# Experts of a hybrid decoder: empty slots left out of gather and store, results put at the place of their pair

## The chip, the cores and the metric

One core of a Trainium2 chip runs the whole program. The metric is the device time of one execution in microseconds, the median of the runs shown. TensorE (PE), VectorE (DVE), ScalarE (ACT), GpSimd (POOL) and SyncE (SP) run their own instruction streams and meet at semaphores. SP and ACT issue DMAs through hardware queues, POOL through the software queue; all of them are moved by the core's 16 DMA engines.

## The reference, cut to what matters

Two layers work on a residual stream of 1024 tokens by 1024 numbers, all float32. Each layer is a mixer (latent attention and a gated delta rule in layer 0, retention in layer 1), a residual norm, and a mixture of 32 experts with another residual norm. The change concerns the experts only:

```python
def routed_experts(xt, expert_id, weights, w_gate, w_up, w_down):   # xt (1024, 1024), 2 experts a token
    ...
    counts = jnp.zeros((N_EXPERTS,), jnp.int32).at[flat_e].add(1)
    padded = (counts + MOE_BLOCK - 1) // MOE_BLOCK * MOE_BLOCK         # MOE_BLOCK = 128
    start = jnp.cumsum(counts) - counts
    pstart = jnp.cumsum(padded) - padded
    slot = pstart[e_sorted] + (jnp.arange(n, dtype=jnp.int32) - start[e_sorted])
    ...
    xb = xt[slot_tok].reshape(n_blocks, MOE_BLOCK, D)

    def expert_block(args):
        xs, e = args
        hid = jax.nn.silu(xs @ w_gate[e]) * (xs @ w_up[e])             # 1024 -> 512
        return hid @ w_down[e]                                         # 512 -> 1024

    yb = lax.map(expert_block, (xb, block_expert)).reshape(n_slots, D)
    contrib = yb[slot] * w_sorted[:, None].astype(yb.dtype)
    return jax.ops.segment_sum(contrib, tok_sorted, num_segments=T)
```

So 2048 pairs of token and expert are computed, each weighted and added to its token.

## The kernel before, in words

`build` runs the stages one after the other; each is a block of its own that ends with a barrier of all engines. `moe` (line 2598 on) runs four of them for each layer, tagged f0 and f1: `modulate`, `route`, `experts`, `combine`.

`route` (line 2001) computes the logits, picks the two experts of each token and gives each pair a slot. Slots come in blocks of 128; block e belongs to expert e, and blocks 32 to 47 are spare for experts with more than 128 pairs. The slots of a block are filled from its first one. Then 16 pairs of one-hot tiles A and B, each with a matmul into pk (line 2075), put token + 1 at the place of its slot: pk has the slot within the block on its partition and the block on its column; an empty slot holds 0. From it DVE makes `full` (does the block hold more than 64 rows, line 2193), and `token` (line 2194 on), where an empty slot asks for token 0. `route`'s SP loads the first experts' weights beside that.

`experts` (line 2239) walks over the blocks in groups of four (QUAD), as many as `used` says. For a block v:

- SP loads gate and up weights (`load_gu`, lines 2224 and 2225, 2 MB each) into one of four buffers, then the down weights of block v - 3 (`load_d`, line 2229, two times 1 MB) into one of two buffers.
- POOL (`gather`, lines 2323 and 2326) copies the column of tokens and issues an indirect DMA that fetches 128 rows of x, 4 KB each, into one of two buffers, once the transposes of block v - 2 are through.
- PE runs gates(v), hid_turn(v - 1), turn(v + 1), downs(v - 1), in this order. turn transposes the gathered rows, gates multiplies by gate and up, hid_turn transposes the hidden rows, downs multiplies by the down weights. gates and downs work on two halves s of 64 rows; the second is left out where `full` is 0. Within a half, the two column halves of the result lie on partitions 0 to 63 and 64 to 127.
- ACT and DVE apply the modulation (lines 2441 and 2488), the Silu, the product, and copy the down projection into y (128 x 2 x 512; ACT line 2457 for s = 0, DVE line 2509 for s = 1). So y[64 c + t, s, :] is columns 512 c on of the row 64 s + t.
- ACT waits for both copies and stores y with two DMAs of 256 KB (line 2461) at the block's place in y_dram (`expert_rows`).

`combine` (line 2533) reads, for each tile of 128 tokens, the two rows of each token from y_dram with indirect DMAs from POOL (line 2555, four tiles of buffers), multiplies them on PE by diagonal weights (line 2579), and ends with the residual norm: DVE lines 1598 to 1624, ACT, and on POOL the bias (line 1643). POOL asks for tile t + 4 ahead of its own work on tile t. SP loads x and stores the result (`traffic`, in order: x of tile t, then the store of tile t - 3 once its bias is added).

`attention` (line 788), in layer 0, also stores zeros over the 16 spare blocks of y_dram (lines 826 and 831), so that they can be read.

## Time and profile before

| | us |
|---|---|
| median of the runs | 3794.65 |
| lowest and highest of 3 runs | 3790.22 and 3802.92 |
| the profiled execution | 3790.52 |
| its span, first to last instruction | 3788.7 |
| experts of layer 0, first to last PE instruction, about | 1201 to 1798 |
| experts of layer 1, the same | 3109 to 3698 |
| PE busy over the span | 3229.5 (85%) |

How the rows are read. In a row of the slices, each digit is the busy share of a slice of 94.7 us in tenths. A row of the groups has line, engine, operation, output<-inputs, size, count, then busy us, mean ns of one, idle time of the engine before them and who ended it. A row of busy times by stretch has the stretch, its length, then busy us and count of PE, PE's weight loads, DVE, ACT and POOL, the granted clock as a share of full speed, the DMA engines' mean busy share and GB/s. A row of the timeline has start, length, engine, line, what was done, count, and in brackets the idle time before it and who ended that. A row of the DMA issues has the issuing queue, the count, KB each and the median us from issue to landing. A matmul of float32 appears as two records.

### The profile page before, as it was taken

Reading aid. Unit: us, or ns where it says so; the run is one execution under the profiler, and the core shown is the slowest. Engines: PE = TensorE matmul, PEld = TensorE weight load, DVE = VectorE, ACT = ScalarE, POOL = GpSimd, SP = SyncE. Lnnn points to the kernel's source line nnn. Section 1 sums busy time; section 2 is a strip of 40 time slices with the busy share of each in tenths; the row PEclk is TensorE's granted clock in tenths of the full one; section 3 lists DMA queues with packets and bytes.
Section 4 is the critical chain, followed back from the end, with each engine's and each line's share of the span. In section 5 each row is a group of like instructions: output and inputs, shape, how many; then the busy total and the mean of one; then the engine's idle time right before and its main releaser. Section 6 shows DMA issues by size and latency. Waiting matters only on the chain. (4 is left out here: it accounts for less than half of the span.)

```text
span 3788.7 us, 44646 instructions
## 1 busy us (share of the span) xinstructions
PE 3229.5 (85%) x15035; PEld 1782.1 (47%) x15036; DVE 1274.6 (34%) x3073; ACT 908.2 (24%) x1749; POOL 503.7 (13%) x866
## 2 busy tenths in 40 slices
PE   7978889677865999999479899999989759988884
PEld 5656654367434434333146565655644343433331
DVE  4665554354243112221623232232311241121226
ACT  1022224123120111111135354453410011111111
POOL 0000010166010000000301111111100100000003
PEclk9879999778885999999689999999989859999997
DMA  7722001122235999996530202010030157899985
GB/s 283 270 87 84 0 23 34 49 65 47 89 104 230 388 367 411 425 426 236 214 111 1 67 0 67 0 45 22 0 122 34 60 230 300 329 427 424 426 358 200
DMA packets 195570, 668.26 MB, mean 176 GB/s; under 512 B 46863, under 2 KB 97770, under 8 KB 162414
## 3 DMA queue, kind: packets, MB, share of 16 engines
q1 hardware_dynamic: 162574, 579.56, 39.5%
q0 software_dynamic: 14144, 51.39, 3.5%
q10 hardware_dynamic: 18720, 35.66, 2.5%
q8 instruction: 70, 1.15, 0.1%
q14 instruction: 62, 0.51, 0.0%
HBM read 605.17 MB, written 61.37 MB: 176 GB/s over the span
## 5 line engine op out<-in xcount | busy, mean ns | idle before, releaser
L1805 PE MATMUL ret_pqkv<-ret_w,hT_mix 128*128 128x512 f32 x1024 | 457.6, 600 | 20.0 <-DMA ret_w<-in_ret_w_in_dram 20.0
L2354 PE MATMUL f0e_pgu<-f0w_gu,f0e_xT 128*64 128x512 f32 x1568 | 344.8, 596 | 7.0 <-issue 3.2
L1678 PE MATMUL mo_py<-mo_w,mixT 128*128 128x512 f32 x768 | 333.4, 597 | 4.8 <-DMA mo_w<-in_ret_w_out_dram 2.5
L1805 PEld LDWEIGHTS ret_pqkv<-ret_w,hT_mix 128*128 128x128 f32 x1024 | 192.6, 193 | 240.1 <-issue 239.9
L2354 PE MATMUL f1e_pgu<-f1w_gu,f1e_xT 128*64 128x512 f32 x1344 | 296.0, 595 | 7.4 <-issue 3.6
L1678 PEld LDWEIGHTS mo_py<-mo_w,mixT 128*128 128x128 f32 x768 | 147.0, 192 | 192.6 <-issue 184.8
L1813 PE MATMUL ret_pgate<-ret_w,hT_mix 128*128 128x256 f32 x1024 | 231.6, 379 | 0.0
L2354 PEld LDWEIGHTS f0e_pgu<-f0w_gu,f0e_xT 128*64 128x64 f32 x1568 | 125.4, 138 | 220.9 <-issue 220.8
L2373 PE MATMUL f1e_pd<-f1w_d,f1e_hidT 128*64 128x512 f32 x672 | 173.1, 668 | 52.6 <-DMA f1w_d<-in_moe_w_down_dram 51.3
L1813 PEld LDWEIGHTS ret_pgate<-ret_w,hT_mix 128*128 128x128 f32 x1024 | 189.9, 190 | 25.0 <-issue 1.9
L2354 PEld LDWEIGHTS f1e_pgu<-f1w_gu,f1e_xT 128*64 128x64 f32 x1344 | 104.2, 138 | 194.1 <-issue 194.0
L2373 PE MATMUL f0e_pd<-f0w_d,f0e_hidT 128*64 128x512 f32 x784 | 176.9, 600 | 7.4 <-DMA f0w_d<-in_moe_w_down_dram 5.5
L434 PE MATMUL gc_pq<-hT_mix,gc_w 128*128 128x512 f32 x384 | 168.3, 597 | 10.1 <-DMA gc_w<-in_hy_w_in_dram 10.1
L1960 DVE TENSOR_TENSOR ret_state<-ret_state,ret_pout 128x256 f32<-128x256 f32 x56 | 23.5, 421 | 406.2 <-PE ret_pout L1837 406.2
L2502 DVE COPY f0e_hidT<-f0e_ph 128x512 f32<-128x512 f32 x32 | 22.1, 691 | 363.7 <-PE f0e_ph L2366 363.3
L2502 DVE COPY f1e_hidT<-f1e_ph 128x512 f32<-128x512 f32 x32 | 22.1, 691 | 359.0 <-PE f1e_ph L2366 359.0
L1790 POOL TENSOR_TENSOR ret_z<-ret_z,ret_head_gain 128x256 f32<-128x256 f32 x64 | 46.5, 726 | 700.5 <-DVE ret_z L1971 700.5
L2373 PEld LDWEIGHTS f1e_pd<-f1w_d,f1e_hidT 128*64 128x64 f32 x672 | 53.0, 153 | 149.4 <-issue 93.5
L434 PEld LDWEIGHTS gc_pq<-hT_mix,gc_w 128*128 128x128 f32 x384 | 73.4, 192 | 102.3 <-issue 91.9
L1879 ACT COPY ret_v<-ret_pqkv 128x256 f32<-128x256 f32 x64 | 23.8, 372 | 389.1 <-PE ret_pqkv L1805 389.1
L1598 DVE TENSOR_TENSOR mo_z<-mo_py,mo_gate_b 128x1024 f32<-128x1024 f32 x16 | 19.6, 1225 | 272.0 <-PE mo_py L1678 272.0
L2373 PEld LDWEIGHTS f0e_pd<-f0w_d,f0e_hidT 128*64 128x64 f32 x784 | 58.3, 138 | 102.7 <-issue 94.2
(547 smaller groups left out, 4705.4 us busy)
## 6 DMA issues: line engine op xcount, KB each, us to landing
f0w_gu<-in_moe_w_gate_dram SPq DMA_DIRECT2D x32, 2048.0 KB, 11.3
f0w_gu<-in_moe_w_up_dram SPq DMA_DIRECT2D x32, 2048.0 KB, 16.8
f0w_d<-in_moe_w_down_dram SPq DMA_DIRECT2D x64, 1024.0 KB, 15.8
f1w_gu<-in_moe_w_gate_dram SPq DMA_DIRECT2D x32, 2048.0 KB, 25.5
f1w_gu<-in_moe_w_up_dram SPq DMA_DIRECT2D x32, 2048.0 KB, 30.5
f1w_d<-in_moe_w_down_dram SPq DMA_DIRECT2D x64, 1024.0 KB, 24.9
mixT<-in_ada_w_dram SPq DMA_DIRECT2D x80, 512.0 KB, 5.6
expert_rows<-f0e_y ACTq DMA_DIRECT2D x64, 256.0 KB, 10.4
```

The costliest lines, as they stand in the source:

```text
L434: mm = pe.matmul(pq[u][:, half * 512:(half + 1) * 512], w[u][:, kk, :], g.hT[:, kk, half * 512:(half + 1) * 512], start=(kk == 0), stop=(k ...
L1598: dve.tensor_tensor(z[:, :], y, self.gate_b[:, :], ALU.mult).then_inc(S["zmul"], 1)
L1678: mm = pe.matmul(py[t % 3][:, half * 512:(half + 1) * 512], mixT[:, kk, t * P:(t + 1) * P], ws[:, kk, half * 512:(half + 1) * 512], start= ...
L1790: pool.tensor_tensor(zb, zb, head_gain[u][:, :], ALU.mult).then_inc(S["gained"], 1)
L1805: mm = pe.matmul(p_qkv[s % 2][:, :], g.hT[:, kk, t * P:(t + 1) * P], w[u][:, kk, 0:512], start=(kk == 0), stop=(kk == KD - 1))
L1813: mm = pe.matmul(p_gate[s % 2][:, 0:RDV], g.hT[:, kk, t * P:(t + 1) * P], w[u][:, kk, 512:W], start=(kk == 0), stop=(kk == KD - 1))
L1879: act.copy(v[b][:, :], p_qkv[s % 2][:, QK:512])
L1960: ch.mark(dve.tensor_tensor(st[:, :], state[(s - 1) % 2][:, :], p_out[:, RDV:2 * RDV], ALU.add))
L2354: mm = pe.matmul(pgu[s][half * HALF:(half + 1) * HALF, :], xT[u % 2][:, kk, s * HALF:(s + 1) * HALF], ew.gu[u][:, :, kk, half * FH:(half + ...
L2373: mm = pe.matmul(pd[s][half * HALF:(half + 1) * HALF, :], hidT[:, s, k % 2, k // 2, :], ew.d[u % 2][:, k, half * DH:(half + 1) * DH], star ...
L2502: dve.tensor_copy(hidT[:, :, :, :, :].rearrange("p s j h t -> p (s j h t)"), ph[:, :])\
```

## The change

`route` numbers the second pair of a token T higher than the first, so that a slot knows its pair (token, or 1024 + token) and not only its token; an empty slot gets an index out of bounds. The tokens for the gather are made from that. PE turns the pairs with four small matmuls, so that each partition of y finds the row and the column half that it belongs to (`dest`, twice the pair plus the half). In `experts`, the gather skips indices out of bounds; the two buffers are set to 0 once ahead of the loop. ACT's two stores go. POOL instead issues, after the gather for block v, two indirect stores for block v - 4, one for each s, with rows of 512 numbers; they too skip indices out of bounds. y_dram has 2048 rows, one for each pair. In `combine` the indirect gathers are plain loads from SP, issued ahead of x of the same tile. The zeros in `attention` go, with their memset.

```diff
@@ attention
-            sp.wait_ge(blanked, 1)
-            for i in spare:
-                sp.dma_start(g.y_dram[i * P:(i + 1) * P, :], blank[:, :]).then_inc(cleared, 16)
-            sp.wait_ge(cleared, 16 * len(spare))
...
-            pool.memset(blank[:, :], 0.0).then_inc(blanked, 1)
@@ route, tensor
+            pe.wait_ge(S["paired"], 1)
+            for s_ in range(2):
+                for c in range(2):
+                    mm = pe.matmul(pl[c * 64:c * 64 + 64, s_ * NBLK:(s_ + 1) * NBLK], g.ident[:, s_ * 64:s_ * 64 + 64],
+                                   pairf[:, :], start=True, stop=True, skip_group_check=True)
+            mm.then_inc(S["dealt"], 1)
@@ route, vector
-            ch.do(dve.tensor_copy(tok[:, :], tok_i[:, :]))
+            ch.do(dve.tensor_copy(tok[:, 0, :], tok_i[:, :]))
+            ts(tok[:, 1, :], tok[:, 0, :], float(T), None, ALU.add)
+            ts(low_half[:, :], tok[:, 0, 0:1], P // 2 + 0.5, None, ALU.is_gt)
...
             ts(r.full[:, :], pk[64:65, 0:NBLK], 0.5, None, ALU.is_gt)
-            ch.do(dve.memset(tokf[:, :], 0.0))
-            ts(tokf[:, 0:NBLK], pk[:, 0:NBLK], -1.0, 0.0, ALU.add, ALU.max)
+            ts(pairf[:, :], pk[:, 0:NBLK], 0.5, float(4 * PAIRS), ALU.is_lt, ALU.mult)
+            dve.scalar_tensor_tensor(out=pairf[:, :], in0=pk[:, 0:NBLK], scalar=-1.0, in1=pairf[:, :],
+                                     op0=ALU.add, op1=ALU.add).then_inc(S["paired"], 1)
+            dve.wait_ge(S["paired"], 1)
+            ch.do(dve.memset(tokf[:, :], float(4 * PAIRS)))
+            ts(tokf[:, 0:NBLK], pairf[:, :], T - 0.5, float(-T), ALU.is_gt, ALU.mult)
+            tt(tokf[:, 0:NBLK], tokf[:, 0:NBLK], pairf[:, :], ALU.add)
             ch.do(dve.tensor_copy(r.token[:, :], tokf[:, :]))
+            dve.wait_ge(S["dealt"], 1)
+            ts(r.dest[:, :, :].rearrange("p s n -> p (s n)"), pl[:, 0:2 * NBLK], 2.0, low_half[:, 0:1], ALU.mult, ALU.add)
@@ experts, gpsimd
                 pool.indirect_dma_start(out=xg[b][:, :], out_offset=None, in_=x_dram,
-                                        in_offset=bass.IndirectOffsetOnAxis(ap=idx[b][:, :], axis=0))\
+                                        in_offset=bass.IndirectOffsetOnAxis(ap=idx[b][:, :], axis=0),
+                                        bounds_check=T - 1, oob_is_err=False)\
                     .then_inc(pairs["x_in"][b], 16)
+            def scatter(m, u, dst):
+
+                k, b = turns(m, u, 0)
+                pool.wait_ge(S["ya"], m * QUAD + (u + 1))
+                pool.wait_ge(S["yb"], m * QUAD + (u + 1))
+                reach(pool, pairs["stored"][b], k * 32)
+                pool.tensor_copy(didx[b][:, :], dst).then_inc(pairs["didxd"][b], 1)
+                pool.wait_ge(pairs["didxd"][b], k + 1)
+                pool.sem_inc(S["asked"], 1)
+                for s in range(2):
+                    pool.indirect_dma_start(out=yd, out_offset=bass.IndirectOffsetOnAxis(ap=didx[b][:, s:s + 1], axis=0),
+                                            in_=y[b][:, s, :], in_offset=None, bounds_check=2 * PAIRS - 1, oob_is_err=False)\
+                        .then_inc(pairs["stored"][b], 16)
+
+            for b in range(2):
+                pool.memset(xg[b][:, :], 0.0).then_inc(S["blanked"], 1)
+            pool.wait_ge(S["blanked"], 2)
             for u in range(QUAD):
                 gather(0, u, tk[:, 0:1, u])
             with pool.Fori(1, quads_used(pool)) as m:
                 for u in range(QUAD):
                     gather(m, u, tk[:, bass.ds(m, 1), u])
+                    scatter(m - 1, u, dest[:, bass.ds(m - 1, 1), u, :].rearrange("p a s -> p (a s)"))
             end = quad_last(pool)
             gather(end + 1, 0, tk[:, bass.ds(end + 1, 1), 0])
+            for u in range(QUAD):
+                scatter(end, u, dest[:, bass.ds(end, 1), u, :].rearrange("p a s -> p (a s)"))
@@ experts, scalar
-                act.wait_ge(S["ya"], m * QUAD + (u + 1))
-                act.wait_ge(S["yb"], m * QUAD + (u + 1))
-                for c in range(2):
-                    act.dma_start(yd[bass.ds(k, 1), b, c].rearrange("a t s n -> (a t) s n"),
-                                  y[b][c * HALF:(c + 1) * HALF, :, :]).then_inc(pairs["stored"][b], 16)
@@ combine
-            rn.traffic(sp)
+            def load_rows(t):
+                if t >= NR:
+                    sp.wait_ge(summed, t - NR + 1)
+                for k in range(2):
+                    sp.dma_start(rows[k][t % NR][:, :], y_dram[k * T + t * P:k * T + (t + 1) * P, :])\
+                        .then_inc(r_in[t % NR], 16)
+
+            for t in range(NT + 3):
+                if t < NT:
+                    load_rows(t)
+                    rn.load_x(sp, t)
+                if t == 1:
+                    rn.load_rows(sp)
+                if t >= 3:
+                    rn.store(sp, t - 3)
+            sp.wait_ge(rn.S["stored"], 16 * NT)
...
-                    pool.indirect_dma_start(out=rows[k][t % NR][:, :], out_offset=None, in_=y_dram,
-                                            in_offset=bass.IndirectOffsetOnAxis(ap=r.slot[:, t, k:k + 1], axis=0))\
-                        .then_inc(r_in[t % NR], 16)
@@ build
-    g.y_dram = nc.dram_tensor("expert_rows", [NBLK * P, D], F32).ap()
+    g.y_dram = nc.dram_tensor("expert_rows", [PAIRS, D], F32).ap()
```

## Rows read from the trace of the kernel before

**Rows 1.** The slices of the page: the DMA engines.

```profile
DMA  7722001122235999996530202010030157899985
```

**Rows 2.** The groups of instructions: the down projections of layer 0 and layer 1.

```profile
L2373 PE MATMUL f0e_pd<-f0w_d,f0e_hidT 128*64 128x512 f32 x784 | 176.9, 600 | 7.4 <-DMA f0w_d<-in_moe_w_down_dram 5.5 <-DVE f0e_hidT L2502 1.3
...
L2373 PE MATMUL f1e_pd<-f1w_d,f1e_hidT 128*64 128x512 f32 x672 | 173.1, 668 | 52.6 <-DMA f1w_d<-in_moe_w_down_dram 51.3 <-DVE f1e_hidT L2502 1.0
```

**Rows 3.** Busy times by stretch, one in layer 0 and two in layer 1.

```profile
1600.00:1700.00 100.00, 99.66 (x490) 40.17 (x488) 20.17 (x48) 16.45 (x41) 6.90 (x12) 1.00 1.01 425
3210.00:3310.00 100.00, 98.93 (x478) 39.46 (x475) 14.32 (x33) 11.83 (x30) 4.61 (x8) 1.00 0.84 333
3310.00:3670.00 360.00, 305.84 (x1405) 120.00 (x1405) 74.49 (x176) 60.42 (x154) 25.29 (x44) 0.93 1.00 422
```

**Rows 4.** The timeline of PE in layer 1: two down projections that follow one another.

```profile
3576.11 5.35 PE L2373 MATMUL f1e_pd<-f1w_d,f1e_hidT 128*64 128x512 f32 x16 [3.62 <-DMA f1w_d<-in_moe_w_down_dram]
...
3593.36 5.32 PE L2373 MATMUL f1e_pd<-f1w_d,f1e_hidT 128*64 128x512 f32 x16 [3.45 <-DMA f1w_d<-in_moe_w_down_dram]
```

**Rows 5.** The DMA issues: weights and stores of layer 1's experts, x of its combination.

```profile
f1w_gu<-in_moe_w_gate_dram SPq DMA_DIRECT2D x32, 2048.0 KB, 25.5
...
f1w_d<-in_moe_w_down_dram SPq DMA_DIRECT2D x64, 1024.0 KB, 24.9
...
expert_rows<-f1e_y ACTq DMA_DIRECT2D x64, 256.0 KB, 9.1
...
f1c_x<-x SPq DMA_DIRECT2D x8, 512.0 KB, 4.5
```

**Rows 6.** The timeline at the end of layer 1's route.

```profile
3103.30 1.09 PE L2075 MATMUL f1r_pk<-f1r_B,f1r_A 128*128 128x48 f32 x4 [0.17 <-DVE f1r_B L2178]
...
3107.41 0.20 DVE L2090 TENSOR_SCALAR f_full<-f1r_pk 1x48 int32<-1x48 f32 x1
...
3108.07 0.19 DVE L2196 CAST f_token<-f1r_tokf 128x52 int32<-128x52 f32 x1
```

**Rows 7.** The timeline: the memset in attention, and the first gather of layer 1's experts.

```profile
280.37 0.95 POOL L831 MEMSET at_blank<- 128x1024 f32 x1 [273.52 <-POOLq L94]
...
3110.29 1.02 POOL L2326 DMA_INDIRECT f1e_xg<-x,f1e_idx  x1 [0.84 <-POOL f1e_idx L2323]
...
3122.10 1.97 PE L2348 MATMUL f1e_px<-ident,f1e_xg 128*128 128x128 f32 x8 [9.06 <-DMA f1e_xg<-x,f1e_idx]
```

**Rows 8.** The tiles f1e_y (stores), then f1e_xg (gathers): time from issue to landing.

```profile
DMA to landing us min/median/max: 3.1/9.1/14.0
...
DMA to landing us min/median/max: 4.2/11.1/12.3
```

**Rows 9.** The timeline at the end of layer 1's experts and the start of the combination.

```profile
3699.27 1.42 ACTq L2461 DMA_DIRECT2D expert_rows<-f1e_y  x2
...
3706.49 0.81 SPq L1545 DMA_DIRECT2D f1c_x<-x  x2
```

**Rows 10.** The timeline of layer 1's combination: PE, DVE's first step of tiles, SP.

```profile
3708.33 3.78 PE L1572 MATMUL f1c_py<-f1c_diag,ones 128*128 128x512 f32 x4 [9.95 <-DVE f1c_diag L1565]
3718.73 19.55 PE L2579 MATMUL f1c_py<-f1c_r,f1c_weights 128*128 128x512 f32 x40 [6.62 <-DMA f1c_r<-expert_rows,f_slot]
...
3724.58 1.23 DVE L1598 TENSOR_TENSOR f1c_z<-f1c_py,f1c_gate_b 128x1024 f32<-128x1024 f32 x1 [13.17 <-PE f1c_py L2579]
...
3733.14 1.22 DVE L1598 TENSOR_TENSOR f1c_z<-f1c_py,f1c_gate_b 128x1024 f32<-128x1024 f32 x1
...
3741.31 0.34 SPq L1550 DMA_DIRECT2D out_dram<-f1c_z  x1
...
3745.43 1.22 DVE L1598 TENSOR_TENSOR f1c_z<-f1c_py,f1c_gate_b 128x1024 f32<-128x1024 f32 x1
...
3755.23 1.22 DVE L1598 TENSOR_TENSOR f1c_z<-f1c_py,f1c_gate_b 128x1024 f32<-128x1024 f32 x1 [3.06 <-PE f1c_py L2579]
...
3768.78 1.22 DVE L1598 TENSOR_TENSOR f1c_z<-f1c_py,f1c_gate_b 128x1024 f32<-128x1024 f32 x1 [1.26 <-PE f1c_py L2579]
```

More of the change, by code:

```diff
@@ L804, in attention @@
         otok = g.sb(ctx, "at_o", [P, NT, 2 * VD])
-        blank = g.sb(ctx, "at_blank", [P, D])
-        blanked, cleared = g.sems(ctx, "at", "blanked", "cleared")
-        spare = range(NE, NBLK)
         nmax = g.sb(ctx, "at_nmax", [P, NI])
@@ L1989, in __init__ @@
         self.weight = g.sb(ctx, f"{tag}_weight", [P, NT, 2])
-        self.slot = g.sb(ctx, f"{tag}_slot", [P, NT, 2], I32)
+        self.dest = g.sb(ctx, f"{tag}_dest", [P, 2, NBLK], I32)
         self.token = g.sb(ctx, f"{tag}_token", [P, NBLK + QUAD], I32)
@@ L2012, in route @@
         iota = sb("iota", [P, P])
-        tok = sb("tok", [P, NT])
+        tok = sb("tok", [P, 2, NT])
+        low_half = sb("low_half", [P, 1])
+        slot = sb("slot", [P, NT, 2], I32)
+        pairf = sb("pairf", [P, NBLK])
         gm, gs, gi, m1, m2, i1, i2, ex, tw = (sb(n, [P, NT]) for n in "gm gs gi m1 m2 i1 i2 ex tw".split())
@@ L2037, in route @@
         pk = g.ps(ctx, f"{tag}_pk", [P, 512])
-        names = "w_in b_in iotas logits steps grp gexp diff dexp onehot ranked hit placed".split()
+        names = "w_in b_in iotas logits steps grp gexp diff dexp onehot ranked hit placed paired dealt".split()
         S = dict(zip(names, g.sems(ctx, tag, *names)))
@@ L2249, in experts @@
         idx = [sb(f"idx{u}", [P, 1], I32) for u in range(2)]
+        didx = [sb(f"didx{u}", [P, 2], I32) for u in range(2)]
         xg = [sb(f"xg{u}", [P, D]) for u in range(2)]
@@ L2259, in experts @@
         pd = [g.ps(ctx, f"{tag}_pd{s}", [P, 512]) for s in range(2)]
-        names = "xt_a xt_b xa xd gu_a gu_b silu_a silu_b hid_a hid_b ht hTd down_a down_b ya yb asked left".split()
+        names = "xt_a xt_b xa xd gu_a gu_b silu_a silu_b hid_a hid_b ht hTd down_a down_b ya yb asked left blanked".split()
         S = dict(zip(names, g.sems(ctx, tag, *names)))
-        pairs = {n: g.sems(ctx, tag, n + "0", n + "1") for n in "idxd x_in stored".split()}
+        pairs = {n: g.sems(ctx, tag, n + "0", n + "1") for n in "idxd didxd x_in stored".split()}
         block = ctx.enter_context(nc.Block())
@@ L2546, in _ @@
         def _(sp):
-            rn.traffic(sp)
+            def load_rows(t):
[13 more added lines that the diff above has]
+            sp.wait_ge(rn.S["stored"], 16 * NT)
         @block.gpsimd
         def _(pool):
-            def gather(t):
-                if t >= NR:
-                    pool.wait_ge(summed, t - NR + 1)
-                for k in range(2):
-                    pool.indirect_dma_start(out=rows[k][t % NR][:, :], out_offset=None, in_=y_dram,
-                                            in_offset=bass.IndirectOffsetOnAxis(ap=r.slot[:, t, k:k + 1], axis=0))\
-                        .then_inc(r_in[t % NR], 16)
-            for t in range(NR):
-                gather(t)
             for t in range(NT):
-                if t + NR < NT:
-                    gather(t + NR)
                 rn.pool(pool, t)
```

11 lines of the change are left out of this document (6 added, 5 removed).

## The prediction, made before the change was run

> **What bounds the kernel now.** I began with the slices of the page: the DMA engines are full in two stretches, late in each layer's experts [rows 1]. The groups of instructions come next. In layer 0 the down projection's matmuls (line 2373) waited 5.5 us for their weights, in layer 1 51.3 us; everything else that the experts' matmuls wait for is a few us [rows 2]. A half of a block is 16 of these matmul records, so 784 are 49 halves and 672 are 42: 32 blocks in each layer, of which 17 and 10 hold more than 64 rows. The busy times by stretch say where the two engines trade places [rows 3]. Between 1600 and 1700 the DMA moves 425 GB/s at a share of 1.01 and PE is busy 99.66 us of 100: both are full. From 3210 to 3310 PE is full and the DMA is not. From 3310 to 3670 the DMA is full (422 GB/s) and PE is idle for 54 us of 360. There the start of a block's down projection follows the one before by 17.25 us, with 3.5 us of it a wait for weights [rows 4]. A block's transfers explain this period: gate and up 2 x 2048 KB, down 2 x 1024 KB, stores 2 x 256 KB [rows 5], and the gather of 128 rows of 4 KB, 512 KB. That is 7168 KB = 7.34 MB, and 7.34 MB / 426 GB/s = 17.2 us. So bytes taken away are worth time in that stretch of layer 1; in layer 0 they are worth at most the 5.5 us.
>
> **How much traffic goes.** 2048 pairs lie in 32 x 128 = 4096 slots, so half of the gathered and of the stored rows are dropped: on average 256 KB + 256 KB of a block's 7168 KB, 7.1%. What that is worth depends on how it falls on the 16 DMA engines. The full slots are always the first of a block, so the dropped rows are the high partitions. If the kept rows spread evenly, the stretch shrinks by 7.1% of 360 us = 25.7 us. If each engine serves fixed partitions, the engines with the low partitions keep their whole gather (no block's first rows are empty), and the weights are complete only when the last engine has its share. The scatter is different: a row of 1024 numbers lies as two halves of 512 on partitions t and 64 + t, and the two column tiles s hold the tokens below and above 64. So its kept rows lie in both halves of the partitions, and an engine drops at least most of s = 1: the store falls by about half on every engine. Then 256 of 7168 KB go, 3.6%, 12.9 us. Below these lies a third bound, nothing, if a dropped row costs an engine what a kept one does. No row shows an indirect transfer with dropped rows. I take the middle, 12.9 us: a wait for a whole tile ends with its last engine, and [rows 3] has all engines full before, so the fullest sets the pace afterwards. For layer 0 I take 5 of the 5.5 us.
>
> The Trainium skill, "DMA: Bandwidth & Descriptors", section "The descriptor swizzle", says that a transfer to 128 partitions puts partitions 0 to 63 on engines 0 to 7 and the rest on 8 to 15, four neighbouring partitions to an engine. By it the gather's saving is all on engines that nobody waits for, and the sum is the one I forecast; without it, it would be some 13 us less. No row before the change shows single engines.
>
> **What is added ahead of the experts.** At the end of route DVE has one instruction more before the pairs are known (two for pairf, where one made tokf), and then PE turns pairf with 4 matmuls, 8 records, while DVE makes the tokens (memset, two more steps, cast). Four records of 48 columns took 1.09 us and DVE's small steps come every 0.24 us [rows 6]. So PE starts three steps (0.75 us) after the first of these, the one for the full flags, needs 2 x 1.09 us, and one more DVE step (dest) follows: with 0.1 us of hand-over some 3.3 us. Before, DVE's last step ended 0.85 us after the flags' began. That is +2.4 us in each layer, 4.8 in all, and nothing covers it, because the stage's barrier waits for DVE. The two early steps on tok and low_half lie under the wait for the logits: nothing.
>
> Then two memsets of 128x1024 stand ahead of the first gather on POOL. One such memset took 0.95 us [rows 7], so the gather is issued 1.9 us later. But the gather took 11.8 us to its first use, beside 4 MB of weights issued with it (9.8 us at 426 GB/s), where 4.2 us is its shortest landing [rows 8]. It shares the engines with weights that run out first, so between 0 and 1.9 us appear. I take 1 us a layer, 2 in all.
>
> **Inside the loop.** POOL gets a second wait, for the y of the block four before, behind which the next gather is queued. That y is copied just after the transposes that release the gather ahead of it, and the next gather waits for transposes a block later, so it is not held up. POOL's work per block grows from 0.97 us plus a copy to three indirect DMAs and two copies, with the pauses ahead of them about 5.3 of 17 us, covered. The y buffers are needed again two blocks (34 us) after the scatter is asked for; the longest landing of a store was 14.0 us [rows 8]. Nothing on both. ACT loses 1.42 us of issuing per block and never was late: nothing.
>
> **The end of the experts.** ACT issues its last stores at 3699.27, the next stage's first instruction comes at 3706.49 [rows 9]. Now POOL copies the indices (0.19), pauses 0.84 as it did ahead of a gather [rows 7], and issues two indirect DMAs of 0.97 with 0.3 between: the second starts 2.1 us after where ACT's first did, that is 1.4 after ACT's second. The shortest landing of a store from ACT was 3.1 us, of an indirect gather 4.2 us [rows 8]: +1.1. Sum 2.5 us a layer, bounds 1 and 8 (a landing like the gather's median of 11.1); I take 2.5 since nothing else moves then. 5 in all.
>
> **The combination.** Before, PE was through with the gate rows at 3712.1 and waited until 3718.73 for rows that POOL had asked for [rows 10]. Direct loads on SP take 0.43 us to issue and 4.5 us to land, as x does [rows 5], so both rows of tile 0 are there at about 3712 and PE begins 6.5 us earlier. Against that stands SP's order. Tile t + 4 used to be asked for by POOL ahead of its own work on tile t; now it stands on SP behind the store of tile t, which waits for that work. DVE begins tile 2 at 3733.14, and the store of tile 0 goes out at 3741.31, 8.2 us later [rows 10]. The store and the two loads are 1.5 MB, some 5.3 us to the last landing (4.5 us for 0.5 MB, and about 1 MB more, less overlap), and PE took 5.85 us for a tile from cold (3718.73 to 3724.58). So DVE has tile 4 19.4 us after it began tile 2, where its own work for two tiles takes 12.3 us (3733.14 to 3745.43): 7.1 us late, once for tiles 4 and 5 and once for 6 and 7. Before, DVE went from tile 0 to tile 7 in 44.2 us, with waits of 3.06 and 1.26 us. Without them 39.9, and with two of 7.1 it is 54.1: 9.9 us lost against 6.5 won, about +3 a layer, 6 in all. The bounds of one layer are -3 (loads land in 3.6 us less each) and +6.
>
> **The attention.** The zeros for the spare blocks go: 16 stores and one memset of 0.95 us that ends before the weights it could delay have landed. The store stream lies beside PE-bound work: nothing, at most 0.5 us gained.
>
> **The sum.** Added: 4.8 + 2 + 5 + 6 = 17.8 us. Saved: 12.9 + 5 = 17.9 us. The profiled execution took 3790.52 us (its span 3788.7), so the same execution would take 3790.4. It was the lower end of the runs, 4.1 us under their median of 3794.65; the after kernel's runs should scatter alike, and halfway between the two bases is 3792.5.
>
> **The rivals.** (a) The dropped rows spread evenly: layer 1 saves 25.7 instead of 12.9, so 3792.5 - 12.8 = 3779.7. For it speaks that the indices are read one by one when the transfer is made, so that what is left could be dealt out. Against it, that both the indices and the tile lie by partition, and that a fixed split by partition is the simplest one that gives the full, even share of [rows 3] for full tiles. The rows can't decide; I give the fixed split the larger part. (b) Slower: a dropped row stays as an entry that an engine must work through at the price of a kept one, in the gather and in the scatter. Then the stretch from 3310 does not shrink, none of the 17.9 us comes, and the 17.8 us of added steps stand: 3810.4. It decides as soon as less than some 6 us are saved in all, for then the sum is above +0.3%. For it speaks only that the transfers' number of instructions and their completion count stay; against it, that the bounds check exists to leave rows out. That the change doesn't do what it says is this case. (c) The mechanism of the forecast, but the combination's reload is quicker and starts cleaner: 6 less, 3786; or the stores' tail longer: 5 more. These lie in the forecast's own range, 3783 to 3803.
>
> **How the numbers follow.** Forecast (middle case) 0.5, (a) 0.3, (b) 0.2. A measurement of this kernel can tell about 0.3%, 11.4 us, from no change: the lines are at 3783.3 and 3806.0. The forecast's case lies within them at 0.40, below at 0.05, above at 0.05. Case (a) sits 3.6 us beyond the lower line, so 0.19 of its 0.3 are faster and 0.11 the same. Case (b) is 0.16 slower and 0.04 the same. Together 0.24, 0.55, 0.21. The range reaches to both rivals: from 3775, a little under (a), since the combination's bound could add, to 3811, just above (b).
>
> **What would show it.** In layer 1, the period of the down projections between 3310 and 3670: 16.6 us in the forecast, 16.0 by (a), 17.2 by (b). The DMA share there: under 1.00 while PE still waits for f1w_d means uneven engines (about 0.96); 1.00 with a shorter stretch means (a); 1.00 and the same length (b). The packets of the software queue: about half of the gathers' 4 KB rows, none of the combination's, and the kept 2 KB halves. PE's wait for f0w_d should be near 0. Route should end 2.4 us later, the combination's first matmul of rows should come some 6 us sooner after the stage's start, with two waits of about 7 us for rows in each combination instead of the smaller ones. The prediction is wrong if the indirect stores hold POOL so long that gathers come late (PE would wait for f1e_xg inside the loop), or if their landings delay the copies of y.

## The result, and the profile after

The changed kernel takes 3819.52 us (median of 7 runs, 3808.09 to 3821.09), the kernel before beside it 3798.05 us (7 runs, 3790.22 to 3802.92). The ratio is 1.005, 95% interval 1.0038 to 1.0062: slower by 0.5%, some 19 us. The prediction, 3792.5 us with a range of 3775 to 3811, was wrong. Scaled to the median from which it was made, the ratio gives 3813.6, also above the range. The profiled execution took 3821.04 us, its span is 3819.3.

The page of the kernel after: the slices of the DMA engines, their packets, and the software queue (packets, MB, share).

```profile
DMA  7720001221235989993530202010030157799954
...
DMA packets 185075, 625.33 MB, mean 164 GB/s; under 512 B 55021, under 2 KB 105928, under 8 KB 151918
...
q0 software_dynamic: 19776, 33.62, 2.4%
```

Before, the packets had 668.26 MB, so 42.9 MB are gone. Two runs below put half of them back one by one: 17.8 MB are gathered rows (fullgather, 51.43 MB in this queue) and 16.8 MB stored rows (fullstore, 50.37 MB); the rest is the 8.4 MB of zeros for the spare blocks. So the rows were left out, and rival (b) can be asked directly: over the whole trace a packet of 4 bytes in this queue took 9 ns, one of 4096 bytes 162 ns in the mean. The groups of the down projections answer to [rows 2]; PE waits less for down weights in both layers, 1.7 us where it was 5.5 and 41.7 where it was 51.3:

```profile
L2409 PE MATMUL f1e_pd<-f1w_d,f1e_hidT 128*64 128x512 f32 x672 | 167.7, 650 | 45.4 <-DMA f1w_d<-in_moe_w_down_dram 41.7
...
L2409 PE MATMUL f0e_pd<-f0w_d,f0e_hidT 128*64 128x512 f32 x784 | 175.3, 596 | 3.6 <-DMA f0w_d<-in_moe_w_down_dram 1.7
```

PE's timeline in the stretch that the DMA bounds, two down projections that follow one another, as in [rows 4]:

```profile
3594.49 5.00 PE L2409 MATMUL f1e_pd<-f1w_d,f1e_hidT 128*64 128x512 f32 x16 [3.11 <-DMA f1w_d<-in_moe_w_down_dram]
3611.19 5.18 PE L2409 MATMUL f1e_pd<-f1w_d,f1e_hidT 128*64 128x512 f32 x16 [3.26 <-DMA f1w_d<-in_moe_w_down_dram]
```

The period is 16.70 us where it was 17.25; the forecast was 16.6. So the gain came. The loss is at the seams. Here is the timeline of the end of layer 1's experts and the start of its combination (GpSimd, SP, PE, VectorE's first step of tiles 0, 2, 4, 6 and 7), beside [rows 9] and [rows 10]:

```profile
3713.92 0.19 POOL L2352 COPY f1e_didx<-f_dest 128x2 int32 x1 [1.93 <-ACT f1e_y L2491]
3714.96 0.98 POOL L2356 DMA_INDIRECT expert_rows<-f1e_y,f1e_didx  x1 [0.86 <-POOL f1e_didx L2352]
3716.24 0.97 POOL L2356 DMA_INDIRECT expert_rows<-f1e_y,f1e_didx  x1 [0.30 <-issue]
3728.37 0.81 SPq L2580 DMA_DIRECT2D f1c_r<-expert_rows  x2
...
3730.14 3.78 PE L1564 MATMUL f1c_py<-f1c_diag,ones 128*128 128x512 f32 x4 [17.09 <-DVE f1c_diag L1557]
...
3733.07 1.17 SPq L2580 DMA_DIRECT2D f1c_r<-expert_rows  x2
3733.71 3.64 PE L2611 MATMUL f1c_py<-f1c_r,f1c_weights 128*128 128x512 f32 x8
...
3737.39 1.22 DVE L1590 TENSOR_TENSOR f1c_z<-f1c_py,f1c_gate_b 128x1024 f32<-128x1024 f32 x1 [4.17 <-PE f1c_py L2611]
...
3751.52 1.23 DVE L1590 TENSOR_TENSOR f1c_z<-f1c_py,f1c_gate_b 128x1024 f32<-128x1024 f32 x1 [5.34 <-PE f1c_py L2611]
...
3759.70 0.34 SPq L1542 DMA_DIRECT2D out_dram<-f1c_z  x1
3760.08 1.25 SPq L2580 DMA_DIRECT2D f1c_r<-expert_rows  x2
...
3765.62 6.51 PE L2611 MATMUL f1c_py<-f1c_r,f1c_weights 128*128 128x512 f32 x8 [10.71 <-DMA f1c_r<-expert_rows]
...
3772.18 1.22 DVE L1590 TENSOR_TENSOR f1c_z<-f1c_py,f1c_gate_b 128x1024 f32<-128x1024 f32 x1 [8.28 <-PE f1c_py L2611]
...
3792.77 1.23 DVE L1590 TENSOR_TENSOR f1c_z<-f1c_py,f1c_gate_b 128x1024 f32<-128x1024 f32 x1 [8.29 <-PE f1c_py L2611]
...
3798.33 1.22 DVE L1590 TENSOR_TENSOR f1c_z<-f1c_py,f1c_gate_b 128x1024 f32<-128x1024 f32 x1
```

Two things are to be seen. The second store of the last block is asked for at 3716.24 and the next stage starts 12.1 us later. And inside the combination VectorE waits three times for rows: 5.34, 8.28 and 8.29 us.

I cut both traces at the same instructions and took the difference after minus before, in us, layer 0 and layer 1:

| from ... to | layer 0 | layer 1 | both | forecast |
|---|---|---|---|---|
| first matmul of route to first transpose of gathered rows | +2.7 | +2.2 | +4.9 | +6.8 |
| from there to the last matmul of the down projections | -3.8 | -11.5 | -15.3 | -17.9 |
| from there to the first instruction of the combination | +7.9 | +7.2 | +15.1 | +5 |
| from there to VectorE's first step of tile 7 | +6.7 | +7.6 | +14.3 | +6 |
| sum | | | +19.0 | -0.1 |

The span grew by 30.6 us. Of the other 11.6 about 5 lie between the last matmul of layer 0's combination and the first of layer 1's route (1180.7 us before, 1185.8 after) and 4.5 ahead of the first route. The changed kernel's variants below have 1180.2 to 1183.5 us for the first of these. For the second, the trace of probe, which runs the kernel before's code up to there, has 1145.0 us where the kernel before has 1136.3. So I take both for scatter of one execution; the sum of the table agrees with the 19 us of the ratio.

The third row has a cause that the profile's views don't show, since they leave out what isn't work. The records as the profiler took them do (start in us, duration in ns). After, at the end of layer 1's experts:

```
  3713.27   5064 Scalar  EVENT_SEMAPHORE   (waits for the landing of the last stores)
  3714.96    977 GpSimd  DMA_INDIRECT
  3715.25   9965 GpSimd  DRAIN
  3716.24    973 GpSimd  DMA_INDIRECT
  3718.40      8 Scalar  DRAIN
```

Before:

```
  3659.50  10062 GpSimd  DRAIN
  3659.72    968 GpSimd  DMA_INDIRECT      (the last gather)
  3700.81   2427 Scalar  EVENT_SEMAPHORE   (waits for the landing of the last stores)
  3703.32      8 Scalar  DRAIN
```

In these records GpSimd's instruction stream ends a block of code with a drain. After, ScalarE has seen all stores landed at 3718.33, 2.1 us after the last was asked for, but GpSimd's drain ends at 3725.22, 9.0 us after, and the next stage's first instruction comes 3.2 us behind it (3728.37). Before, it came 3.3 us behind ScalarE's wait (3703.24, 3706.49): a drain of 10 us began behind the last gather and was over at 3669.56, under 28 us of TensorE work. The stores moved the last software DMA to the end of the stage, and with it the drain.

### The profile page after: what moved, and what is told of

Same layout as the page of the kernel before. It is cut to its first block and busy times, and to the rows that moved or that the text cites. A ratio compares the mean times of both kernels' runs of the same rounds, so it can differ in the third digit from the quotient of the medians.

```text
span 3819.3 us, 44971 instructions
## 1 busy us (share of the span) xinstructions
PE 3236.5 (85%) x15051; PEld 1790.7 (47%) x15052; DVE 1274.7 (33%) x3085; ACT 907.6 (24%) x1749; POOL 614.4 (16%) x1029
## 3 DMA queue, kind: packets, MB, share of 16 engines
q0 software_dynamic: 19776, 33.62, 2.4%
HBM read 605.17 MB, written 52.99 MB: 172 GB/s over the span
## 5 line engine op out<-in xcount | busy, mean ns | idle before, releaser
L1797 PE MATMUL ret_pqkv<-ret_w,hT_mix 128*128 128x512 f32 x1024 | 458.9, 602 | 20.3 <-DMA ret_w<-in_ret_w_in_dram 20.3
L2409 PE MATMUL f1e_pd<-f1w_d,f1e_hidT 128*64 128x512 f32 x672 | 167.7, 650 | 45.4 <-DMA f1w_d<-in_moe_w_down_dram 41.7
```

The source lines that it names most:

```text
L1797: mm = pe.matmul(p_qkv[s % 2][:, :], g.hT[:, kk, t * P:(t + 1) * P], w[u][:, kk, 0:512], start=(kk == 0), stop=(kk == KD - 1))
L2409: mm = pe.matmul(pd[s][half * HALF:(half + 1) * HALF, :], hidT[:, s, k % 2, k // 2, :], ew.d[u % 2][:, k, half * DH:(half + 1) * DH], star ...
```

## The experiments

Three theories. **1**: the end of the experts is late by GpSimd's drain, not by the landing of its stores. **2**: the combination is late because on SP the loads of rows stand behind stores that wait for GpSimd. **3**: the gather's missing rows save nothing, since they all lie on the same high partitions; the whole gain is the halved stores. The rival of the third is that missing rows help wherever they lie.

**tail**: the changed kernel, whose experts' stage ends without the drain; GpSimd's stores are still waited for by their semaphores.

```diff
-        block = ctx.enter_context(nc.Block())
+        block = ctx.enter_context(nc.Block(no_gpsimd_drain=True))
```

> The changed kernel, with one edit: the block of the experts ends without GpSimd's drain of its software DMAs. Theory 1: after the last indirect store POOL's drain holds the barrier, in the changed kernel from 3715.25 to 3725.22 us, although ACT saw the store landed at 3718.34. Then the next stage starts about 7 us sooner after the last down projection, in both layers: some 14 us less than the changed kernel, the time near 3805, ratio to the kernel before about 1.002. Rival: the barrier waits for the stores' landing or for clearing of semaphores; then nothing changes (3819, ratio 1.005).

Measured: 3801.45 us (10 runs), ratio to the kernel before 1.0007 (0.9993 to 1.0022), that is 18 us less than the changed kernel. The timeline of its end of layer 1's experts:

```profile
3705.22 0.97 POOL L2356 DMA_INDIRECT expert_rows<-f1e_y,f1e_didx  x1 [0.86 <-POOL f1e_didx L2352]
3706.49 0.97 POOL L2356 DMA_INDIRECT expert_rows<-f1e_y,f1e_didx  x1 [0.30 <-issue]
3711.84 0.81 SPq L2580 DMA_DIRECT2D f1c_r<-expert_rows  x2
```

From the last issue to the next stage 5.35 us instead of 12.13: 6.8 us in this layer; in layer 0 the time from the experts' last matmul to the combination's first fell from 17.6 to 11.6. Together 13 us of the 15.1; from the last matmul to the combination's first instruction 1.9 and 0.4 us remain over the kernel before. The other 5 of the 18 us lie within the two intervals, some 5 us each. Theory 1 holds: without the drain the next stage again begins 3.3 us after ScalarE has seen the landing (3708.58, 3711.84).

**probe**: the same cause put into the kernel before. Behind the last down projection GpSimd gathers one block that nobody uses, and waits for it.

```diff
             gather(end + 1, 0, tk[:, bass.ds(end + 1, 1), 0])
+            pool.wait_ge(S["ya"], end * QUAD + QUAD)
+            pool.wait_ge(S["yb"], end * QUAD + QUAD)
+            ...
+            pool.indirect_dma_start(out=xg[1][:, :], out_offset=None, in_=x_dram, ...)
+            pool.wait_ge(pairs["x_in"][1], end * 32 + 48)
```

> The kernel before with one thing added: behind the last down projection of each layer GpSimd gathers one more block of 128 rows by an indirect transfer and waits for its landing; nothing uses it. Theory 1 (the end of a block of code waits for GpSimd's drain, which takes about 10 us from the last indirect transfer on): the stage's end moves 7 us back in each layer, as in the changed kernel, median about 3811 (3806 to 3815), ratio 1.0025 to 1.0045, and GpSimd's drain record ends about 10 us after that gather. Rival (only the landing itself counts, about 4 us of which the ordinary stores' landings already cover 2 to 3): 1 to 2 us per layer, median 3800 to 3802.

Measured: 3806.32 us (10 runs), ratio 1.0024 (1.0012 to 1.0036), which is 9.3 us, less than the 14 of theory 1 and more than the rival's 4. In its trace the time from the experts' last matmul to the combination's first of rows went from 20.0 to 25.9 us in layer 0 and from 20.3 to 25.5 in layer 1. The records:

```
  3715.38    943 GpSimd  DMA_INDIRECT      (the added gather)
  3716.28   5281 Scalar  EVENT_SEMAPHORE   (waits for the landing of the last stores)
  3721.40     42 GpSimd  COMPARE_BRANCH    (the added gather has landed)
  3721.55   2840 GpSimd  DRAIN
```

The drain ends at 3724.39, again 9.0 us after the issue of the last indirect DMA. I had priced it by the changed kernel, where that DMA is asked for 3.8 us after the start of the last matmul; here it is 2.1 us. So the end by the drain is 11.1 us after the matmul, where before the stores' landing was seen 5.4 us after it (3697.8 to 3703.24): 5.7 us were to be expected, 5.2 and 5.9 came. Half of it the rival would claim: the ordinary stores landed 2.8 us later beside the added gather, at 3721.56, and the drain ended 2.8 us after that. So probe alone does not part the two causes; tail does. In the changed kernel, where the landing takes 2.1 us, the drain decides.

**rows**: the changed kernel; in the combination SP asks for the rows of tile t + 1 ahead of the store of tile t - 3.

```diff
+            load_rows(0)
             for t in range(NT + 3):
+                if t < NT - 1:
+                    load_rows(t + 1)
                 if t < NT:
-                    load_rows(t)
                     rn.load_x(sp, t)
```

> The changed kernel, with one edit: in the combination SP asks for the rows of tile t + 1 ahead of the store of tile t - 3, not behind it. Theory 2: the reload behind the store is what makes DVE wait 8.3 us twice in each combination (tiles 4 and 6). Then both waits fall to 0 to 3 us, each combination is 10 to 15 us shorter (from its start to DVE's tile 7: 69.9 us in the changed kernel, 62.3 before), and the time is near 3795, ratio 0.998 to 1.000. Rival: the loads themselves are slow (11.1 us from issue to landing for tile 2), because rows, x, gain and bias share one queue; then DVE's waits stay about as long and less than 5 us are won in all.

Measured: 3790.23 us (10 runs), ratio 0.9982 (0.9969 to 0.9995), 29 us less than the changed kernel. The timeline of its combination in layer 1:

```profile
3713.14 1.76 SPq L2580 DMA_DIRECT2D f1c_r<-expert_rows  x4
...
3715.77 0.95 SPq L2580 DMA_DIRECT2D f1c_r<-expert_rows  x2
...
3722.11 1.22 DVE L1590 TENSOR_TENSOR f1c_z<-f1c_py,f1c_gate_b 128x1024 f32<-128x1024 f32 x1 [4.12 <-PE f1c_py L2613]
...
3730.67 1.22 DVE L1590 TENSOR_TENSOR f1c_z<-f1c_py,f1c_gate_b 128x1024 f32<-128x1024 f32 x1
...
3753.37 1.23 DVE L1590 TENSOR_TENSOR f1c_z<-f1c_py,f1c_gate_b 128x1024 f32<-128x1024 f32 x1 [0.95 <-PE f1c_py L2613]
...
3767.81 1.22 DVE L1590 TENSOR_TENSOR f1c_z<-f1c_py,f1c_gate_b 128x1024 f32<-128x1024 f32 x1 [0.17 <-PE f1c_py L2613]
```

Shown are VectorE's first steps of tiles 0, 2, 5 and 7. The waits of 5.34, 8.28 and 8.29 us at tiles 2, 4 and 6 are gone; what is left is 0.95 at tile 5 and 0.17 at tile 7. Tile 7 comes 54.7 us after the stage's start, where it was 70.0 in the changed kernel and 62.3 before. The combination's matmuls of rows take 49.0 and 49.3 us where the changed kernel's take 62.7 and 63.7. Tile 2, too, is cured: its rows are now asked for at 3715.77, 2.6 us after the stage's start, ahead of tile 1's x, gain and bias, and not 4.7 us after it behind them. Theory 2 holds, and with it the other half of that edit: the direct loads let VectorE begin its first tile 9.0 us after the stage's start, where it was 18.1 [rows 9, 10].

**fullgather**: the changed kernel, but an empty slot fetches row 1023 of x. The stores still leave their rows out.

```diff
+            ts(tokf[:, :], tokf[:, :], float(T - 1), None, ALU.min)
```

> The changed kernel, but the empty slots fetch row 1023 instead of being skipped, so that every gather moves 128 rows of 4 KB. Theory 3 (fixed partitions): the engines with the low partitions had a full gather anyway, so the experts of layer 1 take the same time as in the changed kernel, 0 to 3 us more, with the DMA share back at 1.00. Rival, kept rows spread evenly: 3.6% of 360 us, about 13 us more in layer 1.

Measured: 3816.45 us (6 runs), ratio 1.0057 (1.0036 to 1.0078), no different from the changed kernel. Its period, from PE's timeline, is again 16.7 us:

```profile
3594.49 5.20 PE L2410 MATMUL f1e_pd<-f1w_d,f1e_hidT 128*64 128x512 f32 x16 [3.05 <-DMA f1w_d<-in_moe_w_down_dram]
3611.20 5.35 PE L2410 MATMUL f1e_pd<-f1w_d,f1e_hidT 128*64 128x512 f32 x16 [3.08 <-DMA f1w_d<-in_moe_w_down_dram]
```

The experts of layer 1 take 576.8 us (578.7 in the changed kernel). Half of every gather, left out or not, makes no difference where it lies now. (That all fill rows are the same row did not make them cheap: between 3400 and 3650 this queue's packets of 4096 bytes took 160 ns in the mean in both kernels.)

**fullstore**: the other half alone. The gather leaves rows out, but each empty slot's row is stored, to a spare row of its own that nothing reads.

```diff
-            ts(pairf[:, :], pk[:, 0:NBLK], 0.5, float(4 * PAIRS), ALU.is_lt, ALU.mult)
+            ts(pairf[:, :], pk[:, 0:NBLK], 0.5, None, ALU.is_lt)
+            tt(pairf[:, :], pairf[:, :], spare[:, :], ALU.mult)
...
```

> The changed kernel, but the rows of empty slots are stored after all, each to a spare row of its own behind those of the pairs (nothing reads them); the gather still leaves its empty rows out. Theory (all that the experts gained, 11.5 us in layer 1 and 3.8 us in layer 0 up to the last down projection, comes from the halved stores): layer 1's experts go from 578.7 to about 589 us (4.3 MB more at 422 GB/s are 10 us), layer 0's by 3, the median to about 3832 (3827 to 3838). Rival (the gain came from elsewhere, as from the stores leaving ScalarE's queue): experts within 3 us of 578.7, median 3818 to 3823.

Measured: 3831.83 us (4 runs), ratio 1.0089 (1.0073 to 1.0106).

```profile
3587.36 3.65 PE L2413 MATMUL f1e_pd<-f1w_d,f1e_hidT 128*64 128x512 f32 x16 [1.59 <-DMA f1w_d<-in_moe_w_down_dram]
3604.70 3.65 PE L2413 MATMUL f1e_pd<-f1w_d,f1e_hidT 128*64 128x512 f32 x16 [3.71 <-DMA f1w_d<-in_moe_w_down_dram]
```

The period is 17.3 us, what it was before the change, and the experts take 590.3 us in layer 1 (589.1 before the change) and 597.6 in layer 0 (595.3). From the first transpose of gathered rows to the last down projection, the second row of the table, it is 575.8 and 583.4 us, and 575.7 and 582.2 before. The whole gain was in the stores.

**spread**: the changed kernel with its gathered rows dealt over other partitions, so that the empty slots' rows are missing everywhere alike. The transposition was done as a product with a permutation matrix.

```diff
-                        mm = pe.transpose(px[half][:, j * P:(j + 1) * P], xg[b][:, kk:D:KD], g.ident[:, :])
+                        mm = pe.matmul(px[half][:, j * P:(j + 1) * P], xg[b][:, kk:D:KD], g.perm[:, :],
+                                       start=True, stop=True)
...
```

> The changed kernel, with the gathered rows dealt to other partitions: slot 16 a + e goes to partition 64 (e >> 3) + 32 (a >> 2) + 4 (e & 7) + (a & 3), and PE multiplies by the permutation where it multiplied by the identity, so that the result is the same. Theory 3, an engine serves fixed partitions in groups of four, as the page says: then the kept rows now fall evenly on the 16 engines, the fullest engine drops about half of its gather, and layer 1's experts get shorter by another 3.6% of 360 us, 10 to 13 us; the DMA share in the stretch where PE waits rises from 0.95 to 1.00. Rival: the gather was spread evenly already, or nothing was uneven: 0, or 0.5 us more for the added step in route.

Measured: 3955.03 us (5 runs), ratio 1.041 (1.0385 to 1.0435): this run can't decide its question. The groups of instructions, of this kernel and then of the changed one:

```profile
L2392 PE MATMUL f1e_px<-perm,f1e_xg 128*128 128x128 f32 x528 | 130.9, 402 | 10.0 <-DMA f1e_xg<-x,f1e_idx 10.0
L2392 PEld LDWEIGHTS f1e_px<-perm,f1e_xg 128*128 128x128 f32 x528 | 128.2, 334 | 12.4 <-DMA f1e_xg<-x,f1e_idx 11.6 <-issue 0.8
```

```profile
L2384 PE MATMUL f1e_px<-ident,f1e_xg 128*128 128x128 f32 x264 | 36.0, 280 | 10.2 <-DMA f1e_xg<-x,f1e_idx 10.2
L2384 PEld LDWEIGHTS f1e_px<-ident,f1e_xg 128*128 128x128 f32 x264 | 33.1, 195 | 12.6 <-DMA f1e_xg<-x,f1e_idx 11.8 <-issue 0.8
```

A float32 product with a permutation matrix takes two records where a float32 transpose takes one, and each is 1.4 times as long: 95 us more of PE busy time in each layer, which hides what the deal may bring.

**spread2**: the same idea without a load on PE. Slot 32 a + q is gathered to partition 4 q + a, the transpose stays, and the copies that follow it put the columns back in order.

```diff
-                    ins = act.activation(xT[u % 2][:, j, :], px[0][:, j * P:(j + 1) * P], ACT.Identity,
+                    ins = act.activation(dealt(xT[u % 2], j), there(px[0], j), ACT.Identity,
...
+        def dealt(tile, j):
+            return tile[:, j, :].rearrange("p (a q) -> p a q", a=4)
+        def there(bank, j):
+            return bank[:, j * P:(j + 1) * P].rearrange("p (q a) -> p a q", a=4)
...
```

> Again a deal of the gathered rows over other partitions, this time at no cost for TensorE: the slot numbered 32 a + q of a block (a from 0 to 3, q from 0 to 31) is gathered to partition 4 q + a, the transposition stays as it is, and ScalarE's and VectorE's copies of its result put the columns back in the order of the slots. The column of tokens is moved to the same partitions by one small matmul in the route. So the empty slots' rows are missing on all parts of the partitions alike. Theory 3 (gathered rows saved nothing because the missing ones all lay on the same partitions, whose DMA engines idle while the fullest still carry all their rows): layer 1's experts, now 578.7 us, end about 9 us sooner (4.4 MB fewer at 422 GB/s are 10 us), layer 0's 1 to 3 us sooner, route 0.5 us later per layer: median about 3809 (3804 to 3813), ratio to the kernel before 1.002 to 1.004. Rival (bytes of the gather are hidden anyway, or a missing row costs as much as a kept one): layer 1's experts within 3 us of 578.7, median 3818 to 3822.

Measured: 3801.37 us (10 runs), ratio 1.0013 (1.0002 to 1.0023), 18 us less than the changed kernel. PE's timeline:

```profile
3579.54 5.35 PE L2419 MATMUL f1e_pd<-f1w_d,f1e_hidT 128*64 128x512 f32 x16 [2.61 <-DMA f1w_d<-in_moe_w_down_dram]
3595.62 3.65 PE L2419 MATMUL f1e_pd<-f1w_d,f1e_hidT 128*64 128x512 f32 x16 [2.30 <-DMA f1w_d<-in_moe_w_down_dram]
```

The period is 16.1 us; rival (a) of the prediction, the even spread, had 16.0. Layer 1's experts take 563.4 us (578.7), layer 0's 590.6 (593.1): 17.8 us together, more than the 9 and 1 to 3 that I expected. I had counted only the bytes of the full stretch; at its two ends blocks got shorter as well, from 15.7 and 16.6 us to 13.7 and 14.4 at the start, from 13.7 to 12.0 at the end. The 18 us are net of what was added ahead of the experts, 0.7 and 1.2 us. With fullgather this settles theory 3: this kernel and the changed one leave out the same bytes (33.62 MB in the software queue in both), and they are worth nothing on the high partitions and 15 us when dealt evenly. What single engines do no row shows.

The Trainium skill, "DMA: Bandwidth & Descriptors", section "The descriptor swizzle", gives each engine fixed groups of four neighbouring partitions in a transfer to 128 partitions. The deal was laid out by it, and the result agrees.

The stretch's busy times, 250 us of layer 1, from the kernel before, the changed one, fullgather and spread2 (last columns: clock share, DMA share, GB/s):

```profile
3375.00:3625.00 250.00, 212.23 (x984) 82.37 (x980) 48.74 (x115) 41.02 (x104) 16.27 (x29) 0.94 1.01 425
```

```profile
3400.00:3650.00 250.00, 212.40 (x984) 82.01 (x982) 50.74 (x120) 40.83 (x104) 50.05 (x74) 0.94 1.00 416
```

```profile
3400.00:3650.00 250.00, 213.67 (x990) 83.45 (x988) 50.74 (x120) 40.92 (x104) 50.90 (x74) 0.94 1.01 424
```

```profile
3400.00:3650.00 250.00, 220.59 (x1018) 85.24 (x1020) 52.80 (x126) 42.56 (x108) 51.99 (x76) 0.94 1.01 423
```

The changed kernel moves 416 GB/s where fullgather moves 424, at the same pace of blocks. With the rows dealt the rate is back at 423 and PE is busy 8 us more of 250. The gap is larger at the end of the stretch. Here are the same 25 us and the last down projection that waits for weights, of the changed kernel and then of fullgather:

```profile
3650.00:3675.00 25.00, 21.95 (x103) 8.51 (x100) 3.75 (x9) 3.99 (x10) 5.55 (x8) 0.93 0.78 314
...
3678.32 5.35 PE L2409 MATMUL f1e_pd<-f1w_d,f1e_hidT 128*64 128x512 f32 x16 [2.81 <-DMA f1w_d<-in_moe_w_down_dram]
```

```profile
3650.00:3675.00 25.00, 22.08 (x104) 8.68 (x100) 4.09 (x9) 4.30 (x11) 5.55 (x8) 0.93 1.01 423
...
3678.01 3.65 PE L2410 MATMUL f1e_pd<-f1w_d,f1e_hidT 128*64 128x512 f32 x16 [2.91 <-DMA f1w_d<-in_moe_w_down_dram]
```

The DMA is a fifth idle in the changed kernel, and PE waits as long as with a full one. That fits engines that had less to move and are through with the last weights before the others; the trace does not name them.

**both**: tail and rows together.

> The changed kernel with both repairs together: no drain of GpSimd at the end of the experts' stage, and in the combination SP asks for the rows of tile t+1 ahead of the store of tile t-3. If the two are independent, their gains add up: 3819.5 - 18.1 - 29.3 = 3772, ratio to the kernel before about 0.9935. Rival (they overlap, since rows asked for sooner only wait for the same late transfers): 3780 to 3788.

Measured: 3773.11 us (6 runs), ratio 0.9941 (0.9928 to 0.9954). The gains add up (3772 was expected), so the two causes are independent as far as the medians can tell.

**best**: tail, rows and spread2 together.

> All three repairs on the changed kernel: no drain of GpSimd at the end of the experts, the rows of tile t+1 asked for ahead of the store of tile t-3, and the gathered rows dealt 32 a + q to partition 4 q + a. If the deal's gain (18.2 us in the median when it stood alone) adds to the 46.4 us of the other two, the median is 3755 (3750 to 3760), ratio to the kernel before about 0.989, and layer 1's experts take about 563 us. Rival (the 18.2 were partly the scatter of one program's medians, and the stage's own gains of 15.3 and 2.5 are what holds, of which the clock may take back some): 3758 to 3764.

Measured: 3762.59 us (5 runs, 3753.9 to 3763.18), ratio 0.9905 (0.989 to 0.992), faster than both kernels: 34 us under the one before it ran beside, 57 under the changed one. Experts 590.3 and 563.6 us, as spread2 alone. The median came out as the rival had it, 10.5 us under the run both. The deal's 18 us in a median of its own may in part have been scatter. The clock has a share too: the two runs with a mean granted clock of 0.911 took 3753.9 and 3754.7 us, the three with 0.906 or 0.907 took 3762.6 to 3763.2.

## Why the prediction was wrong

**What bounds, and the saving.** Right. The middle case was chosen: the gather saves nothing, the stores half. Period 16.7 for 16.6 forecast, 12.9 us forecast in layer 1 and 11.5 measured, 5 and 3.8 in layer 0. The forecast of the deciding mechanism was confirmed by three runs: fullgather (the gather is worth nothing), fullstore (the stores are worth all), spread2 (spread evenly, the gather too is worth its bytes). Rival (b), a dropped row at the price of a kept one, is refuted by the period and by the 9 ns of a packet of 4 bytes; that the time came out on its side is no merit of its reason. One marker was looser than I had it: I expected a DMA share of 0.96 through the stretch as the sign of uneven engines. Between 3400 and 3650 the share is 1.00 and the rate 416 GB/s instead of 424; the sign itself, a share under 1.00 while PE still waits for f1w_d, stands at the end of the stretch, 0.78 between 3650 and 3675.

**Ahead of the experts.** Somewhat too dear: 6.8 us forecast, 4.9 measured. The timeline of the end of route and of the start of the experts in layer 1, against [rows 6, 7]:

```profile
3131.39 0.20 DVE L2092 TENSOR_SCALAR f_full<-f1r_pk 1x48 int32<-1x48 f32 x1
...
3132.13 0.67 PE L2076 MATMUL f1r_pl<-f1r_pairf,ident 128*64 128x48 f32 x8 [2.51 <-DVE f1r_pairf L2199]
...
3132.98 0.32 DVE L2092 TENSOR_SCALAR f_dest<-f1r_pl,f1r_low_half 128x96 int32<-128x96 f32 x1
...
3134.30 1.84 POOL L2361 MEMSET f1e_xg<- 128x1024 f32 x2 [69.76 <-POOLq L94]
...
3137.32 1.12 POOL L2338 DMA_INDIRECT f1e_xg<-x,f1e_idx  x1 [0.94 <-POOL f1e_idx L2335]
3148.33 1.98 PE L2384 MATMUL f1e_px<-ident,f1e_xg 128*128 128x128 f32 x8 [10.24 <-DMA f1e_xg<-x,f1e_idx]
```

The four matmuls, eight records, took 0.67 us; I had taken 2 x 1.09 from records that waited for one-hot tiles between each other, so that row was a rate of VectorE and not of PE. From the flags to the last step 1.91 us, 1.06 more than before, not 2.4. The memsets cost 1.2 to 1.6 us and not 1: less of them is hidden by the gather's landing.

**Inside the loop.** Right: GpSimd's busy time grew from 503.7 to 614.4 us and no other engine is seen waiting for it inside the loop; PE waited for gathered rows once in each layer, ahead of the first block (10.2 us in layer 1, 9.1 before).

**The end of the experts.** The failed step: 5 us forecast, 15.1 measured. The prediction said: "I take 2.5 since nothing else moves then." The part that was costed is right in the main: the last issue comes 3.8 us after the start of the last matmul, where ScalarE's second came 2.3 us after it, 1.5 us later for 1.4 forecast (its terms, 0.19 + 0.84 + 0.97 + 0.3, give 2.3 us and not the 2.1 that it wrote). The landing takes 2.1 us in layer 1, less than the 4.2 assumed; there block 31 has no row above 64 and the last store moves nothing. In layer 0, whose last block has both halves, it takes 2.3. What was left out is what GpSimd itself does at the end of its stream, which in the trace of before lay under TensorE's work as a record that no view prints. The upper bound of 8 us a layer held (7.9 and 7.2), the value taken did not. Why the drain lasts as long as it does no run shows.

**The combination.** The mechanism was right and its size was not: 6 us forecast, 14.3 measured, and 6.7 and 7.6 us a layer are also over the bound of 6. Gains: VectorE's first tile began 9.1 us sooner in layer 1 (forecast: PE 6.5 sooner; it was 6.9, and tile 0 was also quicker through PE, 3.68 us from start to VectorE for 5.85). Losses: from tile 0 to tile 7 VectorE took 60.9 us, where the forecast had 54.1 and before it was 44.2. The two waits came where they were forecast, 8.3 us each where it had 7.1. A third, 5.34 us at tile 2, was missed: its rows are SP's ninth order, behind 3 MB of rows and x, gain and bias; they landed 11.7 us after they were asked for, not 4.5. The price of an unloaded transfer was used for a loaded queue.

**The sum.** Of the 19.1 us between -0.1 and +19.0, 10.1 are the end of the experts, 8.3 the combination, 2.6 the smaller saving, and 1.9 went the other way. With my own upper bounds in place of the values taken, the two seams would have given 28 for 11 us and a time of 3809.5. The range was built from the rivals alone, and left out that both of these could be at their ends at once.

## What to carry to other kernels

Moving a stage's last DMA to GpSimd's software queue can lengthen the end of the stage: look in the records of the kernel before for how long GpSimd's drain lasts behind its last indirect DMA, and ask what work will still cover it. Rows left out of a transfer need not be worth their bytes: here they were worth nothing on the high partitions and 15 us in layer 1 when dealt evenly, at the cost of one small matmul a layer, since a copy that follows could restore the order. And when loads move from a queue of their own into one with stores, put the load ahead of the store that waits for other engines.

## What the hardware showed that was not expected

GpSimd's drain ends 9.0 us after the issue of the last indirect DMA in both layers of the changed kernel (layer 1: 3716.24 to 3725.22), 9.1 and 9.0 in probe (3715.38 to 3724.39), but 6.3 and 9.8 before the change (1739.71 to 1745.99, 3659.72 to 3669.56), where the last indirect DMA is a gather. So 9 us is no constant, and how long the drain takes behind a given DMA stays open. It is not the landing alone, which is seen 2.1 to 2.3 us after the issue in the changed kernel, nor a fixed time after the drain's own start (2.84 us in probe, 9.97 after). A stage that waits for its landings by semaphores did without it (tail).

A dropped row of an indirect transfer stays as an entry of 4 bytes. The software queue has 7472 packets of 4 bytes in the changed kernel and 3120 in fullgather, and the difference, 4352, is the number of gathered rows left out (66 gathers of 128 rows less 4096). The stores' dropped rows stand in 4062 packets of 8 bytes, which fullgather has too and fullstore and the kernel before have not. Each of these packets took 9 ns, against 162 for 4096 bytes. The page's line on the memory's traffic counts them as if they were full: it says 52.99 MB written in the changed kernel and in fullstore alike, though the latter stores 16.8 MB more.

ScalarE and VectorE took no longer for a copy whose source and target are read and written in another order of the columns: the medians are 456 and 403 ns in spread2, 456 and 402 ns in the changed kernel.
